# Joining the first combine with the first odd stage, and moving two side jobs to earlier stages

## What is computed

```python
for l in range(DEPTH):                       # DEPTH = 2
    mod_lat = silu(c) @ ada_w[l] + ada_b[l]  # and mod_ctx from c_ctx
    sh1, sc1, g1, sh2, sc2, g2 = split(mod_lat, 6)
    h = rms_norm(x, norm1_g[l]) * (1 + sc1) + sh1
    # l = 0: grouped attention | spatial gate; l = 1: neighbourhood attention with a
    # relative-position bias c_rpb | conformer convolution module
    x = x + g1 * (mixer(h @ w_in) @ w_out)
    h2 = rms_norm(x, norm2_g[l]) * (1 + sc2) + sh2
    f = moe_ffn(h2)                          # 16 experts, best 2 of one group of 4
    x = x + g2 * f
```

## Time and profile before

| | us |
|---|---|
| median of 3 runs | 3068.68 (3063.66 to 3072.29) |
| the profiled execution | 3067.87 |
| its span | 3066.1 |

### The profile page before, as it was taken

How to read it: one execution, slowest core, us unless ns; L and a number is a source line. 1 busy time by engine, 2 the same in 40 slices (tenths; PEclk the granted TensorE clock), 3 DMA queues, 4 the chain that set the end, 5 groups by cost and what they waited for, 6 DMA issues and landing times. The chain is left out here.

```text
span 3066.1 us, 31465 instructions
## 1 busy us (share of the span) xinstructions
PE 2389.5 (78%) x10535; PEld 1758.6 (57%) x10536; DVE 1566.4 (51%) x2093; ACT 986.1 (32%) x1305; POOL 610.4 (20%) x599
## 2 busy tenths in 40 slices
PE   5499888899882799999922765995997836999980
PEld 0378655565650588888700554773665735888770
DVE  2255563443423555656444335994773235576754
ACT  1122243334220545545301211112653104455540
POOL 0133302111113100000012654220312321000002
PEclk9999989899995799999955887997998967999995
DMA  9211045312118667766287664665762245687936
GB/s 386 89 42 42 32 152 209 110 32 62 39 41 246 223 222 278 281 240 224 110 347 275 210 196 136 164 182 165 200 172 80 103 176 189 237 304 278 350 137 233
DMA packets 325628, 551.32 MB, mean 180 GB/s; under 512 B 124189, under 2 KB 168715, under 8 KB 319372
## 3 DMA queue, kind: packets, MB, share of 16 engines
q1 hardware_dynamic: 210976, 401.70, 38.3%
q0 software_dynamic: 26032, 85.59, 8.1%
q10 hardware_dynamic: 88508, 62.61, 6.5%
HBM read 438.00 MB, written 126.51 MB: 184 GB/s over the span
## 5 line engine op out<-in xcount | busy, mean ns | idle before, releaser
L2629 DVE TENSOR_TENSOR ex_gu_lo<-mw_gu,ex_gu_hi 128x2048 fp32r<-128x2048 f32 x128 | 287.3, 2287 | 77.8 <-ACT ex_gu_hi L2549 77.7
L2549 ACT ACTIVATE ex_gu_hi<-mw_gu 128x2048 fp32r<-128x2048 f32 x128 | 237.5, 1911 | 121.6 <-DVE ex_y L2676 115.7
L1659 PE MATMUL at_ps_o<-at_pT,at_v_one 128*128 128x512 f32 x336 | 178.6, 613 | 9.5 <-ACT at_total L1439 9.4
L2524 POOL TENSOR_TENSOR ex_at<-ex_slots,ex_nil 128x1 int32<-128x1 int32 x53 | 16.4, 309 | 805.6 <-PE ex_ps_x L2701 800.6
L2707 PE MATMUL ex_ps_g<-ex_gu_hi,ex_xT_hi 128*128 128x512 f32 x408 | 170.0, 417 | 8.2 <-issue 5.2
L2707 PE MATMUL ex_ps_y<-ex_d_hi,ex_hT_hi 128*128 128x512 f32 x408 | 166.7, 408 | 9.4 <-DVE ex_d_lo L2629 8.0
L2629 DVE TENSOR_TENSOR ex_d_lo<-mw_d,ex_d_hi 128x2048 fp32r<-128x2048 f32 x64 | 143.8, 2288 | 53.8 <-ACT ex_d_hi L2549 53.8
L1429 ACT ACTIVATE at_pT<-at_ps_s 128x512 f32<-128x512 f32 x168 | 99.7, 595 | 211.8 <-PE at_ps_s L1652 211.7
L2707 PE MATMUL ex_ps_g<-ex_gu_lo,ex_xT_hi 128*128 128x512 f32 x408 | 165.0, 404 | 0.0
L2707 PE MATMUL ex_ps_g<-ex_gu_hi,ex_xT_lo 128*128 128x512 f32 x408 | 164.7, 404 | 0.0
L2707 PE MATMUL ex_ps_y<-ex_d_hi,ex_hT_lo 128*128 128x512 f32 x408 | 162.0, 397 | 0.0
(11 more groups left out here) (465 smaller groups left out, 5759.3 us busy)
## 6 DMA issues: line engine op xcount, KB each, us to landing
mw_gu<-in_moe_w_gate SPq DMA_DIRECT2D x32, 2048.0 KB, 10.8
mw_gu<-in_moe_w_up SPq DMA_DIRECT2D x32, 2048.0 KB, 15.7
mw_d<-in_moe_w_down SPq DMA_DIRECT2D x32, 2048.0 KB, 7.8
y_d<-ex_y ACTq DMA_DIRECT2D x51, 512.0 KB
mod_mod_w<-in_ada_w SPq DMA_DIRECT2D x24, 1024.0 KB, 11.0
y_d<-at_zero POOLq DMA_DIRECT2D x36, 512.0 KB, 4.9
co_mod_w<-in_ada_w SPq DMA_DIRECT2D x16, 1024.0 KB, 13.8
edge_d<-rows_d ACTq DMA_DIRECT2D x64, 160.0 KB, 3.8
```

The lines of the kernel that those rows point to most:

```text
L1659: nc.tensor.matmul(ps_o[:, :], v_one[:, kt, g:g + 2, :].rearrange("p a d -> p (a d)"), pT[u % 3][:, :], start=(u == plan.first[i, g]), sto ...
L2524: nc.gpsimd.tensor_tensor(at[:, :], slots[:, bass.ds(within(n, most), 1)], nil[:, :], ALU.add).then_inc(S["at_ready"], 1)
L2549: nc.scalar.activation(dst, src, ACT.Copy).then_inc(sem, 1)
L2629: sub = lambda dst, a, b, sem: nc.vector.tensor_tensor(dst, a, as_f32(b), ALU.subtract).then_inc(sem, 1)
```

## The change

Three things are changed.

1. The first combine is no stage of its own. `CombinedNorm`, a `NormStage`, gathers and combines tile i + 2 in round i of `project_tiles`, stores the sum to `x_d` and goes on from it. The square of tile i + 2 stands at the end of ScalarE's round i, ahead of the rounding of tile i + 1. The convolution weights are loaded and split at the start of this stage, through a ring of eight raw buffers that lie in `w_qk.lo`. The gate of the context tiles is loaded in round 5 into the same buffer. `project_heads` gets raw buffers of its own for `w_v`.
2. All three sets of layer 1's modulation are computed in the routing stage of layer 0: 24 loads in a ring of 12, and 12 stores.
3. The bias rows are masked and the tables copied in the even attention (`BiasRows`): a mask with every second step's values on GpSimd, up to step 62, and a copy after each exponential of the steps 40 to 135 on ScalarE. What a mask and a copy do is the same as before.

The second combine is unchanged in what it does.

```diff
+class CombinedNorm(NormStage):
+    def __init__(self, ph, k, l, tiles, src_of):
+        NormStage.__init__(self, ph, k, l, tiles, src_of, True)
...
+    def gather(self, pool, i):
+        p = i % 2
+        if i >= 2:
+            pool.wait_ge(self.xn_done, i - 1)
+            pool.wait_ge(self.stored[p], 16 * (i // 2))
+        for j in range(2):
+            pool.indirect_dma_start(self.y[j][p][:, :], None, self.k.y_d, bass.IndirectOffsetOnAxis(self.k.dest[:, j, i:i + 1], 0)
+                                    ).then_inc(self.y_in[j][p], 16)
+
+    def combine(self, dve, i):
+
+        nc, k, p = self.nc, self.k, i % 2
+        a, b, turn = self.y[0][p][:, :], self.y[1][p][:, :], 16 * (i // 2 + 1)
+        dve.wait_ge(self.y_in[0][p], turn)
+        nc.vector.tensor_scalar(a, a, k.weight[:, 0, i:i + 1], None, ALU.mult).then_inc(self.weighed, 1)
+        dve.wait_ge(self.y_in[1][p], turn)
+        dve.wait_ge(self.weighed, i + 1)
+        nc.vector.scalar_tensor_tensor(b, b, k.weight[:, 1, i:i + 1], a, ALU.mult, ALU.add).then_inc(self.mixed, 1)
+        dve.wait_ge(self.gate_in, 32 if i >= LT else 16)
+        dve.wait_ge(self.mixed, i + 1)
+        nc.vector.tensor_tensor(b, b, self.gate[:, :], ALU.mult).then_inc(self.gated, 1)
+        dve.wait_ge(self.x_in[p], turn)
+        dve.wait_ge(self.gated, i + 1)
+        nc.vector.tensor_tensor(b, b, self.x[p][:, :], ALU.add).then_inc(self.summed, 1)
+
+    def store(self, sp, i):
+        sp.wait_ge(self.summed, i + 1)
+        sp.dma_start(self.k.x_d[i * P:(i + 1) * P, :], self.y[1][i % 2][:, :]).then_inc(self.stored[i % 2], 16)
+
+    def square(self, act, i):
+        act.wait_ge(self.summed, i + 1)
+        if i:
+            act.wait_ge(self.sq_done, i)
+        if i >= 2:
+            act.wait_ge(self.ms_done, i - 1)
+        self.nc.scalar.activation(self.junk[:, :], self.y[1][i % 2][:, :], ACT.Square,
+                                  accum_out=self.ss[:, i % 2:i % 2 + 1]).then_inc(self.sq_done, 1)
+
+    def scale(self, dve, i):
+        dve.wait_ge(self.rstd_done, i + 1)
+        self.nc.vector.tensor_scalar(self.x[i % 2][:, :], self.y[1][i % 2][:, :], self.rstd[:, i % 2:i % 2 + 1], None,
+                                     ALU.mult).then_inc(self.xn_done, 1)
...
-def conv_weights(ph, w_in):
-
-    return SplitWeights(ph, "w", KD, 2 * BW, lambda i: w_in[i * P:(i + 1) * P, 3 * BW:5 * BW])
+def conv_weights(ph, w_in, o):
+
+    raw = ph.alias("raw", o.w_qk.lo, [P, 8, BW])
+    return SplitWeights(ph, "w", KD, 2 * BW, lambda i: w_in[i * P:(i + 1) * P, 3 * BW:5 * BW],
+                        raw=[raw[:, i, :] for i in range(8)], ring=8)
...
+                ns.load_gate(sp, 0)
                 ns.load(sp, 0)
                 ns.load(sp, 1)
                 ns.load_columns(sp)
-                sp.wait_ge(R["zero"], 2)
-                for i in range(2):
-                    sp.dma_start(bias_rows[i][:, P // 2 - 16:P // 2 + 15], rpbs[i].rearrange("h r c -> (h r) c")).then_inc(R["bias_in"], 16)
                 o.w_qk.load(sp, 0, 2)
+                ns.store(sp, 0)
+                ns.store(sp, 1)
                 for i in range(NT):
                     if i + 2 < NT:
                         ns.load(sp, i + 2)
@@ -766,24 +806,35 @@
                         sp.dma_start(k.hT_d[i, n], as_f32(src[i % 2][:, :, :])).then_inc(h_out[i % 2], 16)
                     if i + 1 < LT:
                         o.w_qk.load(sp, 2 * i + 2, 2 * i + 4)
+                    if i + 2 < NT:
+                        ns.store(sp, i + 2)
+                    if i + 3 == LT:
+                        ns.load_gate(sp, 1)
                 for p in range(2):
                     sp.wait_ge(h_out[p], 16 * NT)
+                    sp.wait_ge(ns.stored[p], 16 * NT // 2)
 
             @block.scalar
             def _(act):
-                act.dma_start(taps_in[:, :], dw).then_inc(S["taps_in"], 16)
+                w.load(act, 0, 8)
+                act.dma_start(taps_in, dw).then_inc(S["taps_in"], 16)
                 for j, src in enumerate((dw_b, ln_g, ln_b)):
                     act.dma_start(o.cols[:, j, :], src.rearrange("(c p) -> p c", p=P), allow_slow_non_contiguous=True
                                   ).then_inc(S["cols_in"], 16)
-                ns.square(act, 0)
+                for n in range(len(w.pieces)):
+                    w.round_hi(act, n, n + 1)
+                    if n and n + 7 < len(w.pieces):
+                        w.load(act, n + 7, n + 8)
+                    if n == 5:
+                        ns.square(act, 0)
                 act.wait_ge(S["zero_ready"], 2)
                 for i in range(NT + 1):
                     if i < NT:
                         if i >= 2:
                             act.wait_ge(h_out[i % 2], 32 * (i // 2))
                         ns.round_hi(act, i)
-                    if i + 1 < NT:
-                        ns.square(act, i + 1)
+                    if i == 0:
+                        ns.square(act, 1)
                     if i < LT:
                         o.w_qk.round_hi(act, 2 * i, 2 * i + 2)
                     if 0 < i <= LT:
@@ -795,57 +846,34 @@
                         act.wait_ge(S["yT_full"], i)
                         nc.scalar.activation(o.yT[:, :, HALO + j * P:HALO + (j + 1) * P], ps_yT[:, :, :], ACT.Copy
                                              ).then_inc(S["yT_done"], 1)
-                    if i == 5:
-                        for p in range(2):
-                            act.wait_ge(R[f"out{p}"], 16 * NP // 2)
-                    if 5 <= i < 9:
-                        o.copy_tables(act, k, 5 * (i - 5), 5 * (i - 4))
+                    if i + 2 < NT:
+                        ns.square(act, i + 2)
                 act.wait_ge(S["cols_in"], 48)
 
             @block.gpsimd
             def _(pool):
...
+                ns.gather(pool, 0)
+                ns.gather(pool, 1)
                 for a in (0, HALO + SEQ):
                     nc.gpsimd.memset(o.yT[:, :, a:a + HALO], 0.0).then_inc(S["zero_ready"], 1)
                 ns.root(pool, 0)
                 for i in range(NT):
+                    if i + 2 < NT:
+                        ns.gather(pool, i + 2)
                     ns.rest_lo(pool, i)
                     if i + 1 < NT:
                         ns.root(pool, i + 1)
-                    if i == 0:
-                        pool.wait_ge(R["bias_in"], 32)
-                    if i < LT:
-                        for n in range(NP * i // 4, NP * (i + 1) // 4):
-                            mask_rows(n)
-                for p in range(2):
-                    pool.wait_ge(R[f"out{p}"], 16 * NP)
 
             @block.vector
             def _(dve):
+                w.rest_lo(dve, 0, 4)
+                ns.combine(dve, 0)
+                w.rest_lo(dve, 4, 8)
                 ns.mean(dve, 0)
                 ns.scale(dve, 0)
+                w.rest_lo(dve, 8, 12)
+                ns.combine(dve, 1)
+                w.rest_lo(dve, 12)
...
+                    if i + 2 < NT:
+                        ns.combine(dve, i + 2)
                     if i < LT:
                         o.w_qk.rest_lo(dve, 2 * i, 2 * i + 2)
...
-                sp.wait_ge(o.tables_out, 16 * 96)
-                    o.copy_tables(act, k, 20 + 9 * j, 29 + 9 * j)
...
+    def load_skew(self, pool, n):
+        i, part = divmod(n, self.NP)
+        pool.dma_start(self.skew[n % 2][:, :, :].rearrange("p c x -> p (c x)"),
+                       self.skews[i, part * self.PART * P:(part + 1) * self.PART * P].partition_broadcast(8 * 15)
+                       ).then_inc(self.skew_in[n % 2], 16)
+
+    def begin(self, pool):
+        for i in range(2):
+            self.nc.gpsimd.memset(self.bias[i][:, :], 0.0).then_inc(self.zeroed, 1)
+        pool.wait_ge(self.zeroed, 2)
+        for i in range(2):
+            pool.dma_start(self.bias[i][:, P // 2 - 16:P // 2 + 15], self.rpbs[i].rearrange("h r c -> (h r) c")).then_inc(self.bias_in, 16)
+        for n in range(2):
+            self.load_skew(pool, n)
+
+    def mask(self, pool, n):
+        i, part = divmod(n, self.NP)
+        if n == 0:
+            pool.wait_ge(self.bias_in, 32)
+        pool.wait_ge(self.skew_in[n % 2], 16 * (n // 2 + 1))
+        if n >= 2:
+            pool.wait_ge(self.out[n % 2], 16 * (n // 2))
+        self.nc.gpsimd.tensor_tensor(self.rows[n % 2][:, :, :], self.skew[n % 2][:, :, :], bc(self.bias[i][:, :], 1, self.PART), ALU.add
+                                     ).then_inc(self.made, 1)
+        pool.wait_ge(self.made, n + 1)
+        pool.dma_start(self.k.rows_d[i].rearrange("h r c x -> (h r) c x")[:, part * self.PART:(part + 1) * self.PART, :],
+                       self.rows[n % 2][:, :, :]).then_inc(self.out[n % 2], 16)
+        if n + 2 < 2 * self.NP:
+            self.load_skew(pool, n + 2)
...
+    def copy(self, eng, n):
+        o, m = divmod(n, 48)
+        if m == 0:
+            for p in range(2):
```

(30 more changed lines are left out.)

146 lines of the change are left out of this document (55 added, 91 removed).

## The result

| | before | after |
|---|---|---|
| median of the runs, us | 3067.6 (3063.7 to 3072.3) | 3043.0 (3037.1 to 3050.2) |
| profiled execution: time / span, us | 3067.9 / 3066.1 | 3045.2 / 3043.5 |
| even attention, first query load to the routing stage's bias load | 552.8 | 594.7 |
| routing stage of layer 0, to the first load of the experts' slots | 68.7 | 113.2 |
| experts of layer 0 | 539.6 | 538.9 |

The ratio after to before is 0.9925, interval 0.9913 to 0.9936: 24.6 us faster. The forecast was 57. Routing is +44.6, the merged stage -106.0, the even attention +41.9; small differences elsewhere sum to -3.1, and all to the 22.6 by which the spans differ. One term is far off: the even attention, 42 us in place of 12.

What follows compares the result with a forecast made beforehand. Even attention was taken as TensorE-bound with free transfer capacity, the first combine and routing as transfer-bound, the first odd stage as a four-engine chain. 41 - 109 + 12 - 1 = -57 gave 3011 us, range 2995 to 3030 (0.62).

Steps and rivals of the forecast that it cites:

- Routing stage, +41: Routing stage of layer 0: 16.8 MB of added modulation weights at 416 GB/s, 40 us, plus 1 for row stores.
- Merged stage, -109: First combine and first odd stage run as one: 216 us in place of 325.4, so 109 us go.
- Body and tail: Merged stage from the turn of tile 1 to the first convolution: 183.2 us before, 172 forecast.
- The head: Merged stage from its beginning to the turn of tile 1: forecast 44 us, ends 38 and 52.
- the first combine again ends at 19.8: Start of the merged stage: first gathers land as before, so the first combine ends 19.8 us in.
- The +7 for the square: Merged stage: squaring a later tile stands ahead of ScalarE's rounding, 1.05 us, seven times, adding 7 us.
- Even attention, +12: Even attention with added masks, skew loads, row stores and table copies: 12 us longer, from -8 to +60.
- GpSimd's +5: Even attention: masks on GpSimd fit its idle time or make due work slightly late in tiles 1 to 3; 0 to +15.
- VectorE's +1 for the lock-out: Even attention, tile 0: GpSimd's masks lock VectorE out for some weight splits; +1 us, 0 to +5.
- The +4 for copies and that stall together: Even attention: copies and masks add bytes beside zero stores, while spreading shortens the query-load stall; +4 us, -9 to +40.
- Rival (a): Even attention: ScalarE's queue fills beside zero stores and holds the exponentials; +40 in place of +4, 3047 us, chance 0.09.
- Rival (c): Even attention: ScalarE pays every copy serially with the exponentials, 1.04 us each, 100 us; kernel 3099, chance 0.03.

## Why the prediction was right and wrong

**Routing stage, +41: right, 44.6.** The stage is 113 us long against the forecast of 110. The reason given was half right: the added bytes go at 420 GB/s where only modulation and expert weights move, but the scatters hold a stretch of 30 us at 237, now 1000 to 1030, in the middle of the 24 loads. The 16.8 MB by 44.6 us are 376 GB/s. SyncE's queue:

```profile
977.31 68.18 SPq L156 DMA_DIRECT2D ro_mod_w<-in_ada_w  x24
```

**Merged stage, -109: right, -106.0.** Body and tail: from the first turn of tile 1 to the first convolution 171.6 us, forecast 172. The scale takes 0.75 us, no rounding waits for a copy, and rounds are 19.7 to 21.3 us, the last four 20.5 to 20.7:

```profile
1674.37 1.94 PE L322 MATMUL pc_pt<-ident,pc_x 128*128 128x128 f32 x8 [14.98 <-DVE pc_x L431]
...
1748.76 0.75 DVE L431 TENSOR_SCALAR pc_x<-pc_y,pc_rstd 128x1024 f32<-128x1024 f32 x1 [3.75 <-POOL pc_rstd L307]
1769.47 0.75 DVE L431 TENSOR_SCALAR pc_x<-pc_y,pc_rstd 128x1024 f32<-128x1024 f32 x1 [3.74 <-POOL pc_rstd L307]
...
1845.98 1.27 DVE L1109 TENSOR_SCALAR po_acc<-cv_yT,cv_taps,cv_cols 128x512 f32<-128x512 f32 x2 [8.73 <-PEq L99]
```

The head is 1674.37 - 1626.53 = 47.8 us, forecast 44 (38 to 52). The step that is off is "the first combine again ends at 19.8": it begins at 20.0 and ends at 24.8, behind four weight splits on VectorE, which wait for ScalarE, which first issues for 16.3 us: eight weight loads, the taps and three slow column vectors.

```profile
1626.54 5.09 ACTq L454 DMA_DIRECT2D cw_raw<-in_od_w_in  x8
...
1635.52 4.50 ACTq L822 DMA_DIRECT2D cv_cols<-in_d_ln_g  x1
...
1642.83 1.15 ACT L461 ACTIVATE cw_w_hi<-cw_raw 128x512 fp32r<-128x512 f32 x2 [25.98 <-issue]
...
1646.48 0.75 DVE L405 TENSOR_SCALAR pc_y<-pc_y,weight 128x1024 f32<-128x1024 f32 x1
```

The +7 for the square was counted as chain time alone; on the chain it is, but the run with the square behind shows that taking it off the chain buys 0.2 us a round, not 1.0.

**Even attention, +12: wrong, 41.9.** This is 30 of the 34 us by which the spans' difference, -22.6, misses the forecast -57; routing and the merged stage add 3 or 4 us each, and small differences elsewhere take some back.
- GpSimd's +5 priced its time, and that costs nothing (556.5 us with the arithmetic, 556.9 without). VectorE's +1 for the lock-out was near the 2.4 us read. What was missing is the transfers of the first 12 masks. They were said to "fit into the 76 us of idle" of GpSimd. GpSimd was idle there, but the transfers met the projection's weight loads, on which ScalarE and VectorE wait in turn with two buffers. The prediction had no term for it; piece 1 measured 14.5 us, some 12 or more of them not VectorE's longer splits. The row that would have shown it is ScalarE's 11.7 us of waits for these loads in the kernel before.
- "Masks now spread these stores, which shortens that stall": the stall on the query load doubled, 9.4 to 19.3. What masks spread in time they also filled up: 7.2 MB of GpSimd's queue in place of 4.7 went beside the load. Of the runs that issue the load late, only those with the zero stores moved away from it lost most of the stall (0.6 us is left with late ones, 1.7 and 3.8 with one every fourth step).
- The +4 for copies and that stall together was by capacity; it measured 26, pieces 2 and 3, of which 16 are held copies. Rival (a) had the mechanism (ScalarE's queue fills and holds the exponentials) and a chance of 0.09. Its price was for 16 copies draining slowly, +40 with no other piece; two copies were held. The "wrong would be" sign, waits for copies' issues on ScalarE, is there. That its time, 3047, lies near the measured 3043 is luck: it priced copies and stall at 40 us, where the runs show 26, and the weight loads at nothing, where they show 14.5. The rule of the Trainium skill ("DMA: Bandwidth & Descriptors", section "Queues, rings and completion order"), turn-taking between queues by packet, pointed the right way: by it a load shares an engine with any other queue that has work at that moment, whatever the mean use. The trace agrees as far as the latency goes (2.9 to 4.4 us); it does not show the turns, and with the engines at 86 to 100% it does not tell them from engines that were full.
- Rival (c), all copies serial with the exponentials, is ruled out: the median issue is 0.54 us, and behind step 64 nothing more is lost.

**`project_heads`, -1:** +1.4, no more than stages with the same code vary between these traces.

So the direction and two of three large terms held. The measured 3043 lies outside the 2995 to 3030 that had a chance of 0.62 and inside the outer ends, 2985 to 3048. The size fell short by one term, the even attention, that was priced by mean DMA use and by GpSimd's idle time, where the transfers' effect on the loads that engines wait for decided.
